# Gates and half of the latent projection as three float32r terms, on a ring of five slots

## What is computed

```python
for i in range(DEPTH):                       # DEPTH = 2
    proj = x @ w_in[i]                       # q, k, v of the neighbourhood attention, latents, rope key, gates
    na_qkv, q_lat, kv_lat, k_rope, g_na, g_mla = split(proj)
    o_na = neighborhood_attention(q_na, k_na, v_na, na_rpb[i])               # 8 heads of 64
    q_mla = rope(rms_norm(q_lat) @ w_uq[i]); kv = rms_norm(kv_lat) @ w_ukv[i]
    o_mla = latent_attention(q_mla, k_mla, v_mla)                            # 8 heads
    merged = sigmoid(g_na + b) * (o_na @ w_na_o[i]) + sigmoid(g_mla + b) * (o_mla @ w_mla_o[i])
    x = layer_norm(ALPHA * x + merged @ w_out[i])
    f = swiglu(x) if i == 0 else moe_swiglu(x)                               # dense FFN, then 8 experts, top 2
    ple = sigmoid(x @ w_ple_gate[i]) * (p[i] @ w_ple[i])
    x = layer_norm(ALPHA * x + f + ple)
```

## Time and profile before

| | us |
|---|---|
| three runs, median (lowest to highest) | 2311.07 (2307.92 to 2311.77) |
| the profiled execution | 2307.82 |
| its span, first to last instruction | 2306.0 |
| PE, DVE, ACT, Pool busy in the span | 2204.6, 1502.4, 980.5, 346.0 |
| granted TensorE clock, mean | 0.973 of full speed |

### The profile page before, as it was taken

The page is one execution under the profiler, slowest core; times in us unless marked ns, Lnnn a source line. Parts: engine busy times, 40 slices in busy tenths (PEclk is TensorE's granted clock), DMA queues, the critical chain, the costliest instruction groups (busy, mean ns, idle before and its releaser), DMA issues.

```text
span 2306.0 us, 29557 instructions
## 1 busy us (share of the span) xinstructions
PE 2204.6 (96%) x11972; PEld 1870.1 (81%) x11972; DVE 1502.4 (65%) x1489; ACT 980.5 (43%) x1043; POOL 346.0 (15%) x95
## 2 busy tenths in 40 slices
PE   8999999989999979999999999999999798969999
PEld 7777899989777868888888888888888586648998
DVE  4342677755333568898888898988889301445776
ACT  0133210010133257777777777778776203241000
POOL 1001200000001112322323223223243000100000
PEclk9999999999999989999999999999999996979999
DMA  9532578643513459999999999999999332303530
GB/s 341 183 124 73 170 268 294 237 132 115 180 60 110 165 209 381 372 384 367 384 367 384 366 385 371 385 374 380 384 387 343 132 135 84 110 0 110 183 128 19
DMA packets 176770, 552.20 MB, mean 239 GB/s; under 512 B 11264, under 2 KB 98944, under 8 KB 133280
## 3 DMA queue, kind: packets, MB, share of 16 engines
q1 hardware_dynamic: 167984, 516.77, 60.9%
q10 hardware_dynamic: 6912, 24.97, 2.7%
q0 software_dynamic: 1776, 9.08, 1.0%
HBM read 527.19 MB, written 23.59 MB: 239 GB/s over the span
## 4 chain that ended last, share of the span: by engine, by line
PE 90%; DVE 6%; ACT 2%; issue 1%; DMA 1%; POOL 0%; DVEq 0%; SPq 0%; ACTq 0%; POOLq 0%
PE act_ps L990 25%; PE act_ps L825 13%; PE dve_ps L1015 12%; PE dve_ps L825 9%; PE dve_ps L918 8%; PE act_ps L918 8%; PE job_ps L951 5%; PE job_ps L825 2%; DVE weights_rest L1884 2%; PE job_ps L877 2%; PE job_ps L998 1%; PE job_ps L888 1%; PE act_ps L1126 1%; ACT expert_short L1414 0%; DVE pre_norm L1673 0%
## 5 line engine op out<-in xcount | busy, mean ns | idle before, releaser
L1884 DVE TENSOR_TENSOR weights_rest<-weight_ring,expert_short 128x2048 fp32r<-128x2048 f32 x280 | 768.2, 2784 | 113.6 <-ACT expert_short L1414 113.6
L1414 ACT ACTIVATE expert_short<-weight_ring 128x2048 fp32r<-128x2048 f32 x336 | 640.8, 1917 | 115.1 <-PE act_ps L990 75.7
L724 POOL TENSOR_TENSOR weights_rest<-weight_ring,expert_short 128x2048 fp32r<-128x2048 f32 x56 | 267.4, 4776 | 685.6 <-ACT expert_short L1414 685.6
L990 PE MATMUL act_ps<-expert_short,tokens_short 128*128 128x512 f32 x896 | 355.1, 396 | 12.0 <-DVE tokens_rest L1894 12.0
L990 PE MATMUL act_ps<-weights_rest,tokens_short 128*128 128x512 f32 x896 | 350.0, 391 | 0.0
L990 PE MATMUL act_ps<-expert_short,tokens_rest 128*128 128x512 f32 x896 | 349.9, 391 | 0.0
L1330 ACT ACTIVATE arena_mla<-act_ps 128x256 f32<-128x256 f32 (+2 forms) x89 | 34.2, 385 | 419.5 <-PE act_ps L918 346.1
L990 PEld LDWEIGHTS act_ps<-expert_short,tokens_short 128*128 128x128 f32 x896 | 168.8, 188 | 46.1 <-issue 12.3
L990 PEld LDWEIGHTS act_ps<-expert_short,tokens_rest 128*128 128x128 f32 x896 | 168.8, 188 | 36.4
L990 PEld LDWEIGHTS act_ps<-weights_rest,tokens_short 128*128 128x128 f32 x896 | 169.0, 189 | 33.7
L1813 DVE TENSOR_TENSOR weights_rest<-weight_ring,ffn_weights_short 128x2048 fp32r<-128x2048 f32 x66 | 151.3, 2293 | 2.3
(11 more groups left out here) (323 smaller groups left out, 3958.3 us busy)
## 6 DMA issues: line engine op xcount, KB each, us to landing
weight_ring<-in_moe_w SPq DMA_DIRECT2D x336, 1024.0 KB, 6.9
weight_ring<-in_w_in SPq DMA_DIRECT2D x44, 1024.0 KB, 7.4
weight_ring<-in_ffn_w SPq DMA_DIRECT2D x32, 1024.0 KB, 7.1
weight_ring<-in_w_out SPq DMA_DIRECT2D x12, 1024.0 KB, 6.9
weight_ring<-in_w_gate SPq DMA_DIRECT2D x11, 1024.0 KB, 5.5
weight_ring<-in_w_up SPq DMA_DIRECT2D x11, 1024.0 KB, 8.0
weight_ring<-in_w_down SPq DMA_DIRECT2D x10, 1024.0 KB, 5.9
weight_ring<-in_w_ple_gate SPq DMA_DIRECT2D x8, 1024.0 KB, 6.8
```

The source lines that it names most:

```text
L724: nc.gpsimd.tensor_tensor(ring_lo[slot][:, half], ring[:, slot, half], shorts[u % SHORTS][:, :], ALU.subtract)\
L990: m = nc.tensor.matmul(bank[0:CAP, :], a[:, 4 * c + k, :], w[:, k, :], start=(c == k == i == 0), stop=(c == 1 and k == 3 and i == 2))
L1414: nc.scalar.activation(shorts[u % SHORTS][:, :], ring[:, slot, half], ACT.Copy).then_inc(moe_w_short, 1)
L1884: V.tensor_tensor(ring_lo[slot][:, half], ring[:, slot, half], shorts[u % SHORTS][:, :], ALU.subtract)\
```

## The change

The gates and the last 512 latent columns of each layer are now made with `split_product` from three float32r terms. Their weights are split in ten "side" units a layer, two of latents and eight of gates, by Pool (cast and subtraction, `split_side`), but for the two first units of layer 0, which ACT casts. The layers' blocks use five slots of the ring (`LAYER_SLOTS`); the sixth holds `in_x`, the seventh the two short pieces `side_w`, so that both live through the attention. The third block's blocks use five slots too, the experts still seven. The first seven expert blocks now wait for the last user of their slot among five, slots six and seven for the last gate tile. Blocks of latents and gates are loaded as two panels of 256 columns. DVE makes `in_x` before all copies of latent tiles. Pool's order changes: the splits of layer 0's latents stand first, the gates' units around the load of the next bias, and layer 1's latent units after layer 0's tail.

```diff
+LAYER_SLOTS = 5
-        in_x = [parts("layer_in_short", "probs", [P, DT, SEQ]), parts("layer_in_rest", "arena_o", [P, DT, SEQ])]
+        in_x = [parts("layer_in_short", "weight_ring", [P, DT, SEQ], SLOT * LAYER_SLOTS),
+                parts("layer_in_rest", "weight_ring", [P, DT, SEQ], SLOT * LAYER_SLOTS + 2048)]
+        side_w = [parts(f"side_weights_short{b}", "weight_ring", [P, 2048], SLOT * (LAYER_SLOTS + 1) + 2048 * b) for b in range(2)]
+        def side_units(l):
+            units = []
+            for u in range(10):
+                block, c = (queries_at[l] - 1, u) if u < 2 else (ple_block_at[l] - 8 + (u - 2) // 2, u % 2)
+                a, d = tiles_before[block]
+                units.append((block, c, (dve_tile_ready, d + 2 * (c + 1)) if u < 2 else (act_tile_ready, a + 2 * (c + 1))))
+            return units
+        gates_read = [side_units(l)[9][2][1] for l in range(LAYERS)]
...
                     if turn == 0:
-                        sp.wait_ge(*blocks[before_moe - SLOTS + b][1])
+                        sp.wait_ge(*(blocks[max(range(b, before_moe, LAYER_SLOTS))][1] if b < LAYER_SLOTS
+                                     else (act_tile_ready, gates_read[1])))
...
             for i in range(1, before_moe):
-                if i >= SLOTS:
-                    sp.wait_ge(*blocks[i - SLOTS][1])
+                if i >= LAYER_SLOTS:
+                    sp.wait_ge(*blocks[i - LAYER_SLOTS][1])
                 load(i)
...
+            def split_side(l, u):
+                units = side_units(l)
+                block, c, _ = units[u]
+                half = slice(c * 2048, (c + 1) * 2048)
+                if (l, u) not in ((0, 0), (0, 1)):
+                    pool.wait_ge(*weights_landed(block))
+                    pool.wait_ge(*(units[u - 2] if u >= 2 else side_units(l - 1)[8 + u])[2])
+                    nc.gpsimd.tensor_copy(side_w[u % 2][:, :], ring[:, slot_of(block), half]).then_inc(side_short, 1)
+                pool.wait_ge(side_short, 10 * l + u + 1)
+                nc.gpsimd.tensor_tensor(ring_lo[slot_of(block)][:, half], ring[:, slot_of(block), half], side_w[u % 2][:, :],
+                                        ALU.subtract).then_inc(side_split, 1)
+            for u in range(2):
+                split_side(0, u)
             pool.wait_ge(consts_loaded, 32)
             pool.wait_ge(*weights_landed(queries_at[0] + 1))
             load_bias(0)
             mask_bias(0)
             for l in range(LAYERS):
-                pool.wait_ge(max_ready, layer_jobs * l + NA_H)
+                if l:
+                    for u in range(2):
+                        split_side(l, u)
+                for u in range(2, 8):
+                    split_side(l, u)
                 if l < LAYERS - 1:
+                    pool.wait_ge(max_ready, layer_jobs * l + NA_H)
                     load_bias(l + 1)
+                for u in (8, 9):
+                    split_side(l, u)
...
-                for i, (c0, c1) in enumerate(lat_blocks(l)):
+                for i, (c0, c1) in enumerate(lat_blocks(l)[:-1]):
                     feature_tiles("D", weights(DT, c1 - c0, landed=l + i > 0), xs,
                                   after=None if i else normed_x(2 * l) if l else first_pieces)
                 pe.wait_ge(in_x_split, l + 1)
+                def side_weights(u):
+                    block, c, _ = side_units(l)[u]
+                    pe.wait_ge(side_split, 10 * l + u + 1)
+                    return tiles(side_w[u % 2][:, :], DT), tiles(ring_lo[slot_of(block)][:, c * 2048:(c + 1) * 2048], DT)
+                for u in range(2):
+                    w = side_weights(u)
+                    for j in range(2):
+                        split_product(dve_bank()[:, 0:SEQ], w, slice(j * P, (j + 1) * P), in_x).then_inc(dve_tile_ready, 1)
+                n.block += 1
...
                 def gate_tile(s):
-                    if s % 4 == 0:
-                        gate_w.append(weights(DT, 512))
-                    product(act_bank()[:, 0:SEQ], cols(gate_w[-1], s % 4 * P, (s % 4 + 1) * P), xs)\
+                    if s % 2 == 0:
+                        gate_w.append(side_weights(2 + s // 2))
+                    split_product(act_bank()[:, 0:SEQ], gate_w[-1], slice(s % 2 * P, (s % 2 + 1) * P), in_x)\
                         .then_inc(act_tile_ready, 1)
...
+            for block, c, _ in side_units(0)[0:2]:
+                act.wait_ge(*weights_landed(block))
+                nc.scalar.activation(side_w[c][:, :], ring[:, slot_of(block), c * 2048:(c + 1) * 2048], ACT.Copy)\
+                    .then_inc(side_short, 1)
```

More of the change, by code:

```diff
@@ L437, in two_panels, with panels_at, dmas @@
             return pair_block(w, w, c0 // 256, c0 // 256 + 1)
+        def panels_at(w, c0):
+            def dmas(slot):
+                return [(tiles(slot[:, i * 2048:(i + 1) * 2048], DT), panel(w, c0 + 256 * i, c0 + 256 * (i + 1))) for i in range(2)]
+            return dmas
         def down_block(w2, g, f_tiles):
@@ L473, in layer_plan @@
             w = t["w_in"][l]
-            out = [(halves(panel(w, COL_LAT + c0, COL_LAT + c1)), "D" * ((c1 - c0) // P)) for c0, c1 in lat_blocks(l)]
+            out = [(halves(panel(w, COL_LAT + c0, COL_LAT + c1)) if i < len(lat_blocks(l)) - 1 else
+                    two_panels(w, COL_LAT + c0), "D" * ((c1 - c0) // P)) for i, (c0, c1) in enumerate(lat_blocks(l))]
             out += [(two_panels(w, COL_Q), "AAAA"), (two_panels(w, COL_K), "DDDD"), (None, "AA"),
@@ L479, in layer_plan @@
                     (None, "DD")]
-            out += [(halves(panel(w, COL_GATE + 512 * i, COL_GATE + 512 * (i + 1))), "AAAA") for i in range(4)]
+            out += [(panels_at(w, COL_GATE + 512 * i), "AAAA") for i in range(4)]
             out += [(halves(panel(t["w_na_o"][l], 0, D)), "D" * DT), (halves(panel(t["w_mla_o"][l], 0, D)), "D" * DT)]
@@ L618, in load @@
                 dmas, _ = blocks[i]
-                for dst, src in dmas(ring[:, i % SLOTS, :]):
-                    sp.dma_start(dst, src).then_inc(weights_here[i % SLOTS], 16)
+                for dst, src in dmas(ring[:, slot_of(i), :]):
+                    sp.dma_start(dst, src).then_inc(weights_here[slot_of(i)], 16)
             def load_expert_block(e, b, base):
@@ L708, in _ @@
                         pool.wait_ge(*units[i - 2][2])
-                        nc.gpsimd.tensor_copy(ff_w[i % 2][:, :], ring[:, block % SLOTS, half]).then_inc(pool_w_short, 1)
+                        nc.gpsimd.tensor_copy(ff_w[i % 2][:, :], ring[:, slot_of(block), half]).then_inc(pool_w_short, 1)
                         pool.wait_ge(pool_w_short, l + 1)
@@ L712, in _ @@
                         pool.wait_ge(act_w_short, 2 * l + i + 1)
-                    nc.gpsimd.tensor_tensor(ring_lo[block % SLOTS][:, half], ring[:, block % SLOTS, half], ff_w[i % 2][:, :],
+                    nc.gpsimd.tensor_tensor(ring_lo[slot_of(block)][:, half], ring[:, slot_of(block), half], ff_w[i % 2][:, :],
                                             ALU.subtract).then_inc(pool_w_split, 1)
@@ L942, in swiglu @@
                     half = slice(c * 2048, (c + 1) * 2048)
-                    short, rest = ff_w[u % 2][:, :], ring_lo[block % SLOTS][:, half]
+                    short, rest = ff_w[u % 2][:, :], ring_lo[slot_of(block)][:, half]
                     if kind == "w2":
@@ L1164, in _ @@
                 w_ple = weights(2, D)
-                p_l = tiles(ring[:, i % SLOTS, 2 * D:2 * D + 2 * SEQ], 2)
+                p_l = tiles(ring[:, slot_of(i), 2 * D:2 * D + 2 * SEQ], 2)
                 def embedding(j0, j1):
```

61 lines of the change are left out of this document (34 added, 27 removed).

## The result

| | before | after |
|---|---|---|
| median of the runs | 2309.49 us (2307.86 to 2311.77, 4 runs beside those of after) | 2345.86 us (2343.85 to 2348.74, 4 runs) |
| ratio to before | 1 | 1.0158, 95% interval 1.0140 to 1.0175 |
| profiled execution: own time, span | 2307.82, 2306.0 | 2346.98, 2345.2 |
| mean granted clock of TensorE | 0.973 | 0.960 |

The account below looks back on a forecast made before the run. TensorE, busy 96% of the span, was taken as the bound. Terms -18.4 - 2.3 + 24.7 + 2.3 + 7 + 1.4 = +14.7 us on the 2311.07 median gave 2326; forecast's own range 2316 to 2340, overall 2297 to 2344.

Parts of the forecast that it names:

- Saving of the gates: Attention: a gate tile falls from 3.46 to 2.88 us, so 32 gate tiles give -18.4 us.
- Phase of Pool's subtraction: Attention: with F the end of an odd step's gate tile, Pool subtracts from F + 2.12 to F + 6.65, holding DVE.
- Its price: Attention: TensorE waits 2.06 us for the probabilities at each of 12 gate units, +24.7 us; bounds 0 to 41.
- Rival (c): Attention: idle time lowers TensorE's granted clock to a mean of 0.8, +32 us, 2358; chance 0.06.
- Start of layer 0: Latents to keys: late split weights and Pool's bias mask make the keys end at 64.6, +2.3 us; bounds 0 to +3.
- Latents of layer 1: Start of layer 1: four cheaper split latent tiles save 2.3 us; the moved split of x is free.
- FFN tail: End of the dense FFN: Pool's two latent units hold DVE, making weights late, +7 us; bounds +3 to +10.
- Short ring ahead of the experts: Expert block 2 waits for the last ple_gate tile, delaying the first expert matmul by 1.4 us; bounds 0 to +5.
- Third block: Experts and the work after them: no added time, 0.
- Rival (a): Attention: Pool's work costs nothing, total -14 us, 2297, faster than before; chance 0.17.
- Rival (b): Attention: half the meetings cost, or 1 us each, +12 us, and 5 for the FFN; about 2311; chance 0.11.
- Rival (d): TensorE waits for Pool's split weights at every unit, or experts starve 20 us by the short ring, 2346; chance 0.05.

Follow-up runs that it names:

- e1: Changed kernel without Pool's subtraction for the gate units, the rounded piece standing in for the rest; 2299.59 us.
- e2: Changed kernel with Pool's gate subtraction within the attention started only after DVE has finished that step's probabilities (line 1818); 2310.49 us.
- e5: Changed kernel with gates computed in float32 as before, while Pool does the same casts and subtractions with a result nobody reads; 2351.46 us.
- e3: Changed kernel with Pool's two latent units of layer 1 begun only when layer 1's input is normalised; 2335.95 us.
- e9: e8 with layer 0's eight latent tiles all in float32 again; 2292.74 us, ratio 0.9922 to the kernel before.
- e11: e9 with Pool beginning layer 1's latent units only when DVE has split layer 1's input; 2287.91 us, ratio 0.9904 to the kernel before.
- e4: Changed kernel's five ring slots and moved input split alone, with gates and all latents in float32 and unsplit as before; 2318.62 us.
- e6: e4 with seven ring slots again for the third block; 2318.70 us.
- e7: Kernel before the change, with its first latent tile computed twice; 2315.23 us.
- e10: Kernel before the change, with its first latent tile computed four times; 2321.76 us.
- e8: Changed kernel with e2's and e3's orders, and layer 0's bias mask after DVE's split of queries, keys and values; 2297.23 us, ratio 0.9943 to before.

## Why the prediction was wrong, point by point

For the second point below: the chain of after behind the first hold of layer 0, and a window there (columns as in the earlier trace rows), with a clock of 0.67.

```profile
129.48 4.35 DVE small L1797
...
136.34 2.00 PE job_ps L931 x4
138.34 5.09 PE act_ps L972 x24
```

```profile
134.60:145.00 10.40, 10.40 (x45) 8.07 (x46) 2.14 (x10) 3.42 (x10) 1.44 (x1) 0.67 0.04 6
```

- **Saving of the gates, -18.4:** right, 9.3 a layer in e1.
- **Phase of Pool's subtraction, line 1797 held to F + 6.7:** right to 0.04 us, and the cause is shown by e1, e2 and e5. **Its price, +24.7, is the step that failed: this term of the sum was mis-sized, and the runs have 36.4.** Five of six holds in an attention left PE idle for 2.03, as worked out (2.06). The other 11.7 us have three parts. The first hold of each attention costs 2.9, as that step has no values to compute, so that DVE's line 1797 comes earlier and was held 4.35: with the 0.03 less at the others, 1.4 more in the two layers. After each hold the turn takes 0.66 instead of 0.44, 12 x 0.22 = 2.6 in the two. And the clock, 7.7: after the first hold scores and gate tile took 2.00 and 5.09 instead of 1.07 and 3.07. The slow pieces, behind two holds in each attention, add to 4.6 in layer 0 (which is 18.98 less 13.05 of waiting, less 1.32) and 3.1 in layer 1 (17.46 - 13.05 - 1.32).
- **Rival (c), the clock:** the prediction took it as all or nothing, at 0.8 for the whole attention. It came as short falls after four of the twelve holds, 7.7 us in the two attentions. The rival ought to have been a term of the sum: each idle time a chance of some us. The earlier trace rows had shown the size of it, 0.55 in a stretch with 3.45 idle in 15 us.
- **Start of layer 0, +2.3:** +2.0, but by chance. PE waited until 26.8, not 25.5, then ran slower for a while, and ended its latents at 40.1 instead of 37.0; the mask held DVE's cast of the first key unit, not its subtraction. Kernels with the same orders there gave +2.0, +2.0, +2.8, +5.0 and +5.3 (after, e1, e3, e2, e5), as the bias landed and the mask met DVE at another place.
- **Latents of layer 1, -2.3:** -2.7. The moved split of x was free, as said, but only while Pool did nothing beside it (e9, e11).
- **FFN tail, +7:** 11.8. The step that failed is the choice between "DVE goes first each time" and "Pool does": Pool did (9.0), and the clock took 2.8. The start of Pool's subtraction, 482.5, doesn't follow from the working: block 39 at 478.2 and a cast of 1.89 give 480.1. It came true (494.18, less the shift of 11.7), because the block landed later and DVE held Pool's cast for 2.95.
- **Short ring ahead of the experts, +1.4:** 2.2 in e4, and +3.7 in after with the clock (the tiles of the router and ple_gate at 4.01, 3.60 and 4.00 instead of 2.17, 3.26 and 3.22). The mechanism, an expert block that waits for the last ple_gate tile, is in the chain.
- **Third block, 0:** +6.5, of the clock (e4, e6, e7 and e10); how much of it the change causes stays open. No bound for it stood in the range. The holds' 11.7, the tail's 4.8, this 6.5 and the 2.3 ahead of the experts are 25.3; with the small terms that came out 0.8 lower, that is the 24.5 between the forecast's 14.7 and 39.2.
- **The range:** the bounds of the terms, added up, give 2293 to 2349 about the median (-17.7 to +38.3), not the 2316 to 2340 of the forecast's own range, for which no working is given. The measured 2345.9 lies inside the bounds and outside the range.
- **Rival (a)**, that Pool's work can be had for nothing, gave 2297 and was refused by the phase; e2 and e8 made it true by choosing the phase (e8's own 2297 is the sum of other terms). **Rival (b)**, half of the meetings, is out: all twelve cost. **Rival (d)** has 2346, the measured time, for a reason that isn't there: PE never waited for a split gate unit.

## What to carry to other kernels

Before work is given to an idle GpSimd, write down at which moments of a step VectorE touches SBUF with something that others wait for, however small, and start GpSimd's long two-operand instruction right after the last of them; here one wait on a semaphore turned +36 us into nothing. A wait of 2 us on TensorE can cost more than 2 us, for the pieces behind it can run at a lower clock: here 13.0 of waiting cost 19.0 and 17.5 in the two attentions, the slower turns included. And compare a changed kernel with the old one stretch by stretch, since a stretch that the change does not touch was up to 6.5 us longer by its clock, 0.3% of this kernel, and the unchanged kernel's own runs lie up to 9.6 us apart. A single run says nothing of differences of that size.

## What the runs showed of the hardware

- A 128x2 tensor_scalar of VectorE, 0.17 us, is held for the whole rest of a GpSimd subtraction (up to 4.35). The Trainium skill ("SBUF — State Buffer", Who interferes with whom) gives the pair of ports to whoever starts first, for the whole instruction; the trace agrees down to this size.
- VectorE's operations that read PSUM ran beside the subtraction at their own time (line 1791: 0.42 at 159.24, inside Pool's 158.81 to 163.38), as the earlier trace rows had it.
- With the same instructions and nearly the same waits, 64 matmuls of the third block took 14.00 us when they began at 1831.93 (before) and at 1845.84 (e10), and 15.34 at a clock of 0.90 when they began at 1832.12 (e7). What decides it stays open.
